# A two-mixer transformer in fp32: stick-breaking weights by a running product of sigmoids, spread over the projections' pieces

## What is computed

```python
z = jnp.einsum('bhqd,bhkd->bhqk', qb, kp) * scale
mask = s_idx < t_idx
log_keep = jnp.where(mask, jax.nn.log_sigmoid(-z), 0.0)
later = lax.cumsum(log_keep, axis=3, reverse=True) - log_keep
a = jnp.where(mask, jnp.exp(jax.nn.log_sigmoid(z) + later), 0.0)
outs.append(jnp.einsum('bhqk,bhkd->bhqd', a, vp))
```

## Time and profile before

| | |
|---|---|
| median of 3 runs | 1518.38 us |
| the profiled execution | 1516.93 us |
| its span in the profile | 1515.2 us |
| mean granted TensorE clock | 0.972 |
| PE busy | 1397.1 us, 92% of the span |
| DVE busy | 928.9 us, 61% |
| ACT busy | 756.1 us, 50% |
| POOL busy | 122.8 us, 8% |
| loads | 231.43 MB, 153 GB/s in the mean |

### The profile page before, as it was taken

How to read it: one execution, slowest core, us unless ns; L and a number is a source line. 1 busy time by engine, 2 the same in 40 slices (tenths; PEclk the granted TensorE clock), 3 DMA queues, 4 the chain that set the end, 5 groups by cost and what they waited for, 6 DMA issues and landing times.

```text
span 1515.2 us, 22764 instructions
## 1 busy us (share of the span) xinstructions
PE 1397.1 (92%) x8786; PEld 1237.3 (82%) x8786; DVE 928.9 (61%) x1328; ACT 756.1 (50%) x1160; POOL 122.8 (8%) x132
## 2 busy tenths in 40 slices
PE   8977999999999899999997899999799788999995
PEld 8956899989987689989886799888589566998883
DVE  5542655547645466555669566677668664767774
ACT  5476544435444355444557255554473464655442
POOL 0011000002400000000004000000004142000000
PEclk9999999999999999999998999999899899999998
DMA  8621555555544345555443344544463012345541
GB/s 289 213 83 34 196 196 182 180 195 176 186 167 167 107 156 197 195 194 178 160 150 112 121 145 144 175 168 167 139 222 112 29 56 83 133 147 168 167 167 56
DMA packets 63309, 231.43 MB, mean 153 GB/s; under 512 B 7024, under 2 KB 7152, under 8 KB 63216
## 3 DMA queue, kind: packets, MB, share of 16 engines
q1 hardware_dynamic: 61632, 224.42, 44.2%
q10 hardware_dynamic: 1584, 5.68, 1.1%
HBM read 229.03 MB, written 1.05 MB: 152 GB/s over the span
## 4 chain that ended last, share of the span: by engine, by line
PE 59%; DVE 24%; ACT 12%; issue 3%; POOL 1%; DMA 0%; DVEq 0%; POOLq 0%; SPq 0%; ACTq 0%
PE ps L515 18%; PE ps L516 17%; PE ps L517 17%; DVE w_lo L1387 11%; ACT w_hi L1015 4%; ACT arena L1098 3%; DVE arena L1547 3%; DVE arena L1542 2%; DVE arena L1444 2%; DVE y_lo L1525 1%; ACT y_hi L1092 1%; PE ps L493 1%; PE ps L792 1%; POOL arena L465 1%; PE ps L939 1%
## 5 line engine op out<-in xcount | busy, mean ns | idle before, releaser
L1387 DVE TENSOR_TENSOR w_lo<-ring,w_hi 128x1024 fp32r<-128x1024 f32 x424 | 511.8, 1246 | 334.9 <-ACT w_hi L1015 334.5
L1015 ACT ACTIVATE w_hi<-ring 128x1024 fp32r<-128x1024 f32 x424 | 427.0, 1053 | 270.9 <-PE ps L517 221.0
L515 PE MATMUL ps<-x_hi,w_hi 128*128 128x256 f32 x1664 | 473.4, 284 | 9.8 <-DVE w_lo L1387 5.7
L516 PE MATMUL ps<-x_lo,w_hi 128*128 128x256 f32 x1664 | 471.5, 283 | 0.0
L517 PE MATMUL ps<-x_hi,w_lo 128*128 128x256 f32 x1664 | 471.4, 283 | 0.0
L515 PEld LDWEIGHTS ps<-x_hi,w_hi 128*128 128x128 f32 x1664 | 319.8, 192 | 16.2 <-issue 9.7
L516 PEld LDWEIGHTS ps<-x_lo,w_hi 128*128 128x128 f32 x1664 | 319.9, 192 | 0.5
L517 PEld LDWEIGHTS ps<-x_hi,w_lo 128*128 128x128 f32 x1664 | 319.9, 192 | 0.0
L515 PE MATMUL ps<-w_hi,y_hi 128*128 128x512 f32 (+1 forms) x624 | 248.7, 399 | 46.3 <-DVE y_lo L1525 21.8
L516 PE MATMUL ps<-w_lo,y_hi 128*128 128x512 f32 (+1 forms) x624 | 243.8, 391 | 0.0
L517 PE MATMUL ps<-w_hi,y_lo 128*128 128x512 f32 (+1 forms) x624 | 243.2, 390 | 0.0
(11 more groups left out here) (213 smaller groups left out, 1341.0 us busy)
## 6 DMA issues: line engine op xcount, KB each, us to landing
ring<-ws SPq DMA_DIRECT2D x424, 512.0 KB, 4.8
tab<-tables ACTq DMA_DIRECT2D x4, 550.0 KB, 5.2
rowg<-rows ACTq DMA_DIRECT2D x3, 512.0 KB, 6.4
h<-x SPq DMA_DIRECT2D x2, 512.0 KB, 4.4
out<-arena SPq DMA_DIRECT2D x2, 512.0 KB, 2.6
arena<-decay ACTq DMA_DIRECT2D x1, 768.0 KB, 7.2
sm<-small ACTq DMA_DIRECT2D x1, 642.0 KB, 8.4
arena<-narrow ACTq DMA_DIRECT2D x1, 296.0 KB, 3.5
```

The source lines that it names most:

```text
L515: mm(o, lh, rh, start=start, stop=False, skip_group_check=True)
L516: mm(o, lh, rl, start=False, stop=False, skip_group_check=True)
L1015: A(w_hi[:, g % RING, c:c + HALF], ring[:, q % RAW, :], ACT.Copy).then_inc(hi_ready, 1)
L1387: V.tensor_tensor(w_lo[:, g % RING, v], ring[:, q % RAW, :], w_hi[:, g % RING, v].bitcast(F32), ALU.subtract).then_inc(lo_ready, 1)
```

## The change

1. **Stick-breaking weights.** Queries now lie on the partitions. ACT takes Sigmoid of the negative score (`sb_keep`) and of the score (`sb_sig`) from PSUM. DVE runs `tensor_tensor_scan` from the last key to the first, once per head of the pair over 384 columns: state times `sb_keep`, then the maximum with `dead`, a table of ones where a key is not before the query. `sb_left` so holds the running product of what is left. One multiplication by `sb_sig`, shifted by one key, gives the weights. POOL masks the diagonal blocks once, PE transposes the six blocks of 128 (`sb_turn`), ACT copies them back to SBUF, and `sb_av` multiplies. Clip, softplus, the sums by triangular matrices, `keep_clock`, and Exp and Ln are gone.
2. **Order in the mixer.** The pieces come in another order (first values of heads 0 to 7, then q and k alternating, the other values as pieces 8 and 9), and the products of a pair stand between or in the middle of pieces. Scores, transposed weights and outputs of a pair share two PSUM banks, two pairs in turn.
3. **Low parts.** `split(g, e)` waits for half a piece. In the FFNs DVE refills the piece before the one at hand (`refill_behind`).
4. **First loads and first norm.** The first norm goes token tile by token tile like the others (`tiles` for `tiles_both`); an ACT copy at the very start brings its table load forward; `narrow`, the rest of `small` and `rowg` are loaded at the end of the mixer, and `narrow` is split inside the first MLP; of the first table only 384 columns are loaded.

```diff
-            def split(g):
-                pe.wait_ge(lo_ready, 2 * g + 2)
+            def split(g, e):
+
+                pe.wait_ge(lo_ready, 2 * g + e + 1)
...
-            def transposed(g, b, first=None):
-
-                split(g)
+            def transposed(g, b, first=None, mid=None):
+
                 s = g % RING
                 for j in range(2):
+                    if j == 1 and mid is not None:
+                        mid()
                     for k in range(KT):
+                        if j == 0 and k % 4 == 0:
+                            split(g, k // 4)
...
-            for t in range(TT):
-                turn_over(0, t)
-            for u in range(8):
...
-            ntri, none = tab[:, C_NTRI:C_NTRI + P], tab[:, C_NONE:C_NONE + P]
+            turn_over(0, 0)
...
+            def sb_turn(p):
+                pe.wait_ge(sb_wmasked, p + 1)
+                for i in range(2):
+                    for j in range(3):
+                        r = nc.tensor.transpose(ps[:, 4 + 2 * (p % 2) + i, j * P:(j + 1) * P],
+                                                sb_a[p % 2][:, i, j * P:(j + 1) * P], ident)
+                r.then_inc(sb_turned, 1)
...
+            def sb_next(p):
+                if p + 1 < 6:
+                    sb_z_(p + 1)
+                sb_turn(p)
+
+            natural(G_SB, (0, 1), first=0)
+            spread(0, 4)
+            transposed(G_SB + 2, 2)
+            transposed(G_SB + 3, 3)
+            pe.wait_ge(sb_v_in, 1)
+            transposed(G_SB + 4, 0)
+            pe.wait_ge(tab_in, 16)
+            sb_z_(0)
+            pe.wait_ge(sb_v_in, 2)
+            transposed(G_SB + 5, 1)
+            sb_next(0)
+            transposed(G_SB + 6, 2, mid=lambda: sb_av(0))
+            sb_next(1)
+            transposed(G_SB + 7, 3, mid=lambda: sb_av(1))
+            sb_next(2)
+
+            def sb_between():
+                sb_next(3)
+
+            natural(G_SB + 8, (0, 1), ((sb_qk, 3), (sb_qk, 4)),
+                    then={(0, 0): lambda: sb_av(2), (0, 1): sb_between, (1, 0): lambda: sb_av(3)})
+            sb_next(4)
+            pe.wait_ge(sb_qk, 5)
+            transposed(G_SB + 10, 2, mid=lambda: sb_av(4))
+            sb_next(5)
+            pe.wait_ge(sb_out_copied, 5)
+            transposed(G_SB + 11, 4, mid=lambda: sb_av(5))
...
+            close([(G_SB + 15, (6, 7))], 1, ((sb_out_copied, 7), (sb_out_copied, 8)))
...
-            def sb_soft(p):
-                e = sb_e[:, p % 3, :, :]
-                act.wait_ge(sb_clipped, p + 1)
-                A(e, e, ACT.Exp).then_inc(sb_exp, 1)
-                act.wait_ge(sb_exp, p + 1)
-                A(e, e, ACT.Ln, bias=1.0).then_inc(sb_log, 1)
...
+            for p in range(6):
+                if p + 1 < 6:
+                    sb_sigmoids(p + 1)
+                sb_copy(p)
+                sb_hi(p)
+                refill(G_SB + 6 + p)
+                if p == 3:
+                    for t in range(TT):
+                        evac(t, G_SB + 9, sb_v[:, t, 512:1024], sb_v_in, scale=rstd[:, t:t + 1])
...
+                dve.wait_ge(sb_kept, p + 1)
+                if p:
+                    dve.wait_ge(sb_weights, p)
+                for i in range(2):
+                    r = V.tensor_tensor_scan(sb_left[:, i, ::-1], sb_keep[p % 2][:, i, ::-1], dead[:, i, :], 1.0,
+                                             ALU.mult, ALU.max)
+                r.then_inc(sb_left_in, 1)
+                dve.wait_ge(sb_left_in, p + 1)
+                dve.wait_ge(sb_taken, p + 1)
+                V.tensor_tensor(sb_a[p % 2][:, :, 0:383], sb_sig[p % 2][:, :, 0:383], sb_left[:, :, 1:384], ALU.mult)\
+                 .then_inc(sb_weights, 1)
...
+                behind = []
+
+                def refill_behind(g):
+
+                    if behind:
+                        refill(behind.pop())
+                    behind.append(g)
...
-                        refill(g)
+                        refill_behind(g)
```

More of the change, by code:

```diff
@@ L530, in transposed, with natural @@
                 r.then_inc(done, 1)
-            def natural(g, banks, waits=(None, None), first=None):
+            def natural(g, banks, waits=(None, None), first=None, then=None):
                 for e in range(2):
-                    split(g + e)
                     s = (g + e) % RING
@@ L549, in natural @@
                                 turn_over(first, 1)
-                    r.then_inc(done, 1)
+                        if t == 1:
+                            r.then_inc(done, 1)
+                        if then is not None and (e, t) in then:
+                            then[e, t]()
             def add(g, tiles, t, k, first, last):
@@ L558, in add, with accumulate @@
                 return r
-            def accumulate(g, tiles, first):
-                split(g)
+            def accumulate(g, tiles, first, mid=None):
                 for k in range(2):
+                    if k == 1 and mid is not None:
+                        mid()
+                    split(g, k)
                     for t in range(TT):
@@ new lines, in _, with pair_banks, sb_sigmoids @@
+            act.wait_ge(scale_done, 1)
+            A(scale, ps[:, 4, 0:T], ACT.Copy).then_inc(scale_ready, 1)
+            for g in range(1, 5):
+                refill(G_SB + g)
+            def pair_banks(p):
+                return ps[:, 4 + 2 * (p % 2):6 + 2 * (p % 2), 0:384]
+            def sb_sigmoids(p):
+                act.wait_ge(sb_z, p + 1)
+                A(sb_keep[p % 2], pair_banks(p), ACT.Sigmoid, scale=-1.0).then_inc(sb_kept, 1)
+                A(sb_sig[p % 2], pair_banks(p), ACT.Sigmoid).then_inc(sb_taken, 1)
@@ new lines, in _ @@
+            sb_sigmoids(6)
+            sb_sigmoids(7)
+            refill(G_SB + 12)
+            refill(G_SB + 13)
+            for p in (6, 7):
+                sb_copy(p)
+                sb_hi(p)
+            refill(G_SB + 14)
+            act.dma_start(narrow_raw, narrow).then_inc(narrow_in, 16)
+            act.dma_start(sm[:, S_CONV:S_TOTAL], small[:, S_CONV:S_TOTAL]).then_inc(rest_loaded, 16)
+            act.dma_start(rowg[:, :], rows[0:1, :].partition_broadcast(P)).then_inc(row_in, 16)
@@ new lines, in _ @@
+            refill(G_SB)
+            dve.wait_ge(scale_ready, SCALE_OF[0] + 1)
+            refill(G_SB + 1)
+            sb_unit(0)
+            refill(G_SB + 2)
+            sb_unit(1)
+            refill(G_SB + 3)
+            sb_unit(2)
+            dve.wait_ge(tab_in, 16)
+            sb_weigh(0)
+            refill(G_SB + 4)
+            sb_unit(3)
+            for p in range(6):
+                if p + 1 < 6:
+                    sb_weigh(p + 1)
+                out_copy(p)
+                refill(G_SB + 5 + p)
+                if p != 2 and p != 3:
+                    sb_unit(4 + (p if p < 2 else p - 2))
@@ L2026, in mixer @@
             rows_(out, r)
[L2028 removed]
+    w = a["w_sb_in"][0]
+    both(w, 2 * D)
+    for u in range(4):
+        if u == 3:
+            both(w, 2 * D + 512)
+        for c in (0, D):
+            cols(w, slice(c + 256 * u, c + 256 * (u + 1)))
+    for r in range(0, D, 256):
+        rows_(a["w_sb_out"][0], r)
     mlp(0)
```

290 lines of the change are left out of this document (116 added, 174 removed).

## The result

The changed kernel takes **1441.67 us** (median of 4 runs, 1439.54 to 1444.97), the kernel before 1517.18 in runs beside it. The ratio is 0.9501, with a 95% interval of 0.9476 to 0.9526: faster, by 75.5 us. The forecast was 1446, in a range from 1436 to 1466. The profiled execution took 1441.61 us with a span of 1439.9.

A forecast was written before the change was run, and what follows sets the result against it. PE was taken as the bound, busy 1397.1 of 1515.2 us, so gains come from its 118 us of idling and its queue. Terms −30.9 − 1.0 − 14.6 − 21.8 − 4.0 = −72.3 gave 1444.6, forecast 1446 us, range 1436 to 1466.

The forecast's parts named there:

- the gap: Stick-breaking mixer, between last projection product and first output product: 52.3 us of short PE work, all predicted to go.
- the closings: End of both FFNs: PE's waits for `y_lo` at the closing products, 21.8 us together, predicted to vanish.
- Part 3: Two FFNs, low part one refill behind: −14.6 for chunk waits, −21.8 for closing waits, −4.0 for half clock behind them.
- the 14.6: Two FFNs: fourteen `w_lo` waits of PE, about 1.0 us per chunk, predicted to go; PE's need taken as 17.6.
- The ring: FFNs: raw transfers predicted just covered, 7.8 against 8.0 us; rival that later landings bind, 1461 or 1487 us, chance 0.10.
- Part 1: Mixer, pairs' work between pieces: −52.3 gap, +18.6 pair products, +4.8 stalls, −2.0 half clock, in all −30.9 us.
- Pair 0's stall of 1.0: Mixer, first pair of heads: 1.0 us charged, its Sigmoid behind a table load with only one piece as cover.
- slack of 1.9 us: Mixer, each pair: weights ready 6.9 us after the piece, PE comes to their transpose at 8.8.
- No half clock any more: Mixer: 2.0 us lost to PE's half-speed clock behind the gap predicted to go, with only short waits left.
- Copies of transposed weights: Mixer: PE waiting for ACT's copies, charged 0.3 us for four pairs and 1.7 for the pair behind piece 9's values.
- Part 2: Kernel start: earlier table load and first product, net −1.0 us, between −3 and +1; moved loads taken as 0.
- The lock: Mixer: rival that POOL's selects and DVE's low parts block each other, 15 us of stall, 1461 us, chance 0.18.

The follow-up runs named there:

- either experiment: Two runs: the changed kernel with direct refill in the FFNs, 1491.69 us; the kernel before with only the refill one piece behind, 1466.23 us.
- selects-first run: The changed kernel with DVE waiting, before the low parts of piece 8, until POOL has masked pair 0: 1438.07 us, ratio 0.9474.

## Why the prediction was right, and where it was not

**The bound.** Right. PE's idle time and the queue in front of it were the right ledger, and the three places named (the gap, the `w_lo` waits, the closings) are where the time came from.

**Part 3, the FFNs: mechanism right, size low.** Predicted −14.6, −21.8 and −4.0, or 40.4; measured 48.9, and 50 by either experiment. By the starts of `down` products, seven chunks took 129.91 us before (926.08 to 1055.99) and 118.86 after (900.82 to 1019.68): 11.05 per FFN, 22.1 for both, against the 14.6. From the last of these starts to the turn-over it was 32.42 before and 19.07 after: 13.35 per FFN, 26.7 for both, against 25.8. So the closings and their half clock were sized right: the 36 last products took 9.97 us before and 8.17 after, 1.8 against the 2.0 charged. The term that failed is the 14.6: I had summed the listed waits, some 1.0 a chunk, but a chunk lost 1.65 us. In the chunk shown above, PE goes 1.33 us from the start of one product to the next at the listed wait (980.15 to 981.48), where 0.12 is normal for that product: 1.21, not 1.05. Another 0.27 are lost at a joint for which no wait is listed (968.19 to 968.69, where 0.23 is normal), and some 0.1 in the first products behind each wait. The step that set PE's need at 17.6 from chunks in which DVE was already behind was wrong: it is 16.98. Period times, not waits, would have given it.

**The ring.** Predicted as just covered, and it was: ACT waited up to 0.95 us for a raw half in a stretch of the FFN (905 to 925 us), landing took 4.8 us, and PE saw nothing of it. This rival is out for the FFNs. In the mixer the raw ring did count: pair 0's Sigmoid stands behind a raw half that was in flight for 5.0 to 6.7 us, and no term of the prediction had that.

**Part 1, the pairs: the gap went as predicted, its filling cost more.** From the first product of weights to the turn-over PE spent 51.25 us outside of pieces before, and 26.35 after. In the after figure 4.31 and 0.82 are waits, 1.2 is the norm's, and 20.0 are the pairs' products: 2.5 each, where 2.32 was predicted (+1.5). The failed terms, against 7.8 us that the mixer fell short:

- *Pair 0's stall of 1.0*: 4.31 (+3.3). 1.9 of that is the block between DVE and POOL. I knew it as a rival, but had let each pair's slack of 1.9 us take it, and pair 0 has no slack: two low parts stand behind its product ready to run, one for each select. The other 1.4 lie ahead of the selects, where the raw half comes late.
- *No half clock any more*: the 2.0 behind the gap went (1.7 by the clock of 136 to 142 us), but 1.7 came back behind pair 0.
- *Pieces cost what they did*: PE's time in pieces is 96.5 us; without the 1.7 behind pair 0 that is 94.8, where before, without the half clock behind the gap, it was 90.2. Part of these 4.6 us lies at the joints: the piece between pairs takes 5.9 to 6.1 us (twice 3.05, from 65.47 to 68.52 and from 69.59 to 72.65), 48 undisturbed products in the FFN 5.7 (0.12 each, as at 917.44 and 917.56). Over the eight pairs that is some 2 us. The rest stays open.
- *Copies of transposed weights*, charged 0.3 four times and 1.7 once: only pair 4 waited, 0.82, so 2.1 came back. The turn-over's wait at the end, 1.48, was 0.79 before: 0.7 for the 0.9.

3.3 + 1.7 + 1.5 + 4.6 − 2.1 − 0.2 is 8.8 of a shortfall of 7.8; where the surplus microsecond lies is not shown. The table load before the first Sigmoid took its 1.28 us with Sigmoid following at once (46.82, 48.11), so there is no further drain, as the row of before said.

**Part 2, the start.** First product at 10.66, predicted 10.6. The loads cost 0. But the earlier start did not shorten the mixer, as the run without the early Copy shows: PE waits for pair 0 either way.

**The rivals.** The lock was real but cost PE time at one pair and not at eight. The middle pairs' selects took 0.77 us; those of pairs 6 and 7 took 2.68, but PE did not wait. The Trainium skill (SBUF — State Buffer, "SBUF: two separate sides") describes an exclusive pair of ports, with the loser blocked for the whole instruction. The trace agrees: each of pair 0's selects took 1.33 to 1.39 us in place of 0.41, so each waited for about one of DVE's two low parts. The scans took 1.81 us for two of 384 columns, as the estimate said.

## What to carry to other kernels

When an engine in the middle of a chain waits for its neighbour's result, give it the piece before: a refill one step behind bought 50 us with three lines. Size such an edit by comparing periods at equal places, since the waits that a profile lists were a third too few. When latency-bound work is spread between streams, look at its first unit by itself: it has no slack, it meets whatever happens to be queued (here two low parts on DVE) or in flight (a raw half), and the clock adds to its stall. What helped in the mixer was to make DVE wait 0.9 us for POOL, and to fill what PE waits for anyway with idle products. And before a microsecond is credited to an edit, look whether something ahead of the edit moved: of the 4.5 us that the selects-first run won, 0.9 had nothing to do with it.

## What the runs showed of the hardware

- Two selects of POOL on 128x256 took 0.77 us alone and 2.68 beside two back-to-back DVE operations with two SBUF operands, each select 0.92 to 0.98 us longer than alone; with DVE held back, 0.77 again. DVE lost only 0.2 us to them (2.56 against 2.36 for two low parts).
- Waits of PE of 2.9 to 5.2 us went with a mean granted clock of 0.50 to 0.68 in the stretches read around or behind them (10 to 14.3 us and 54.6 to 60 us; 0.50 is the lower of the two levels, 1.2 and 2.4 GHz, the rest are mixtures of both), at the start of the kernel as well as in the mixer. With the wait filled by products on ones the clock was 1.00 in both places. With a wait of 1.46 left in the mixer it was 1.00, too. The low clock behind pair 0 cost 1.6 to 2.7 us.
- A table loaded for Sigmoid at the start served Copy as well, with no second load anywhere in the mixer.
